# Second attention and both memory attentions by groups of four units, compressed branch ahead of it

## What is computed

```
# layer 0, per head (12), query tile of 128: keys 0..t, top-k mask
p = softmax(q_rot @ k.T * scale + mask);  o = p @ v
# both layers, memory heads (4), 256 keys, no mask
p = softmax(q_mem @ k_mem.T * scale);     o_mem = p @ v_mem
# layer 1 (NSA), per head (12), 2 groups of key heads
o_c = softmax(q    @ k_cmp.T * scale) @ v_cmp     # 31 compressed keys
o_s = softmax(q_rot @ k_s.T  * scale) @ v_s       # causal, all 8 blocks of 64 selected
o_w = softmax(q_rot @ k_w.T  * scale) @ v_w       # causal window of 512
o   = g0 * o_c + g1 * o_s + g2 * o_w              # g: sigmoid gates
x   = x + concat(o, o_mem) @ w_o
```

## Time and profile before

| | us |
|---|---|
| median of 3 runs (lowest, highest) | 2450.24 (2449.61, 2453.84) |
| profiled execution, its own time | 2453.7 |
| its span, first to last instruction | 2451.9 |
| PE busy | 2407.2 (98%) |
| ACT, POOL, DVE busy | 1070.1, 972.1, 912.3 |
| TensorE clock granted, mean | 0.997 |

### The profile page before, as it was taken

How to read it: one execution, slowest core, us unless ns; L and a number is a source line. 1 busy time by engine, 2 the same in 40 slices (tenths; PEclk the granted TensorE clock), 3 DMA queues, 4 the chain that set the end, 5 groups by cost and what they waited for, 6 DMA issues and landing times.

```text
span 2451.9 us, 36317 instructions
## 1 busy us (share of the span) xinstructions
PE 2407.2 (98%) x12294; PEld 1988.2 (81%) x12294; DVE 912.3 (37%) x1958; ACT 1070.1 (44%) x1853; POOL 972.1 (40%) x484
## 2 busy tenths in 40 slices
PE   8999999999999999999999999999999999999998
PEld 5888888888779978888887878788887797888886
DVE  7965322211567753222114243321211674221212
ACT  6565444422347744344335433432332583432321
POOL 4822444444331124444443413444443423444441
PEclk9999999999999999999999999999999999999999
DMA  4311222233320012322332212232222202232221
GB/s 155 112 36 40 95 98 95 94 103 105 120 69 1 1 45 93 103 94 94 107 107 79 92 38 82 74 103 94 94 96 93 69 18 69 86 103 94 94 95 68
DMA packets 57873, 202.85 MB, mean 83 GB/s; under 512 B 7072, under 2 KB 7968, under 8 KB 57392
## 3 DMA queue, kind: packets, MB, share of 16 engines
q1 hardware_dynamic: 54864, 196.02, 24.2%
q10 hardware_dynamic: 2912, 5.55, 0.7%
HBM read 199.44 MB, written 2.10 MB: 82 GB/s over the span
## 4 chain that ended last, share of the span: by engine, by line
PE 41%; issue 14%; POOL 7%; ACT 1%; DVE 1%; POOLq 0%; DVEq 0%; ACTq 0%
PE bank L804 36%; POOL w_lo L658 7%; PE bank L1058 1%; PE bank L1007 1%; ACT h_hi L1562 1%; PE bank L1442 0%; PE bank L1020 0%; PE bank L1423 0%; PE bank L1437 0%; ACT gained L1565 0%; PE bank L833 0%; ACT tmp L1661 0%; PE bank L838 0%; PE bank L921 0%; PE bank L810 0%
## 5 line engine op out<-in xcount | busy, mean ns | idle before, releaser
L658 POOL TENSOR_TENSOR w_lo<-w_raw,w_hi 128x1024 fp32r<-128x1024 f32 x368 | 883.4, 2401 | 1197.9 <-ACT w_hi L1519 1188.0
L804 PE MATMUL bank<-h_hi,w_hi 128*128 128x512 f32 x1648 | 651.4, 395 | 7.2 <-DVE tmp L2608 1.9
L804 PE MATMUL bank<-h_hi,w_lo 128*128 128x512 f32 x1648 | 643.5, 390 | 0.0
L804 PE MATMUL bank<-h_lo,w_hi 128*128 128x512 f32 x1648 | 643.3, 390 | 0.0
L1519 ACT ACTIVATE w_hi<-w_raw 128x1024 fp32r<-128x1024 f32 x368 | 386.8, 1051 | 241.2 <-PE bank L804 218.2
L804 PEld LDWEIGHTS bank<-h_hi,w_hi 128*128 128x128 f32 x1648 | 310.7, 189 | 82.6 <-issue 6.3
L804 PEld LDWEIGHTS bank<-h_lo,w_hi 128*128 128x128 f32 x1648 | 310.5, 188 | 65.3 <-issue 2.2
L804 PEld LDWEIGHTS bank<-h_hi,w_lo 128*128 128x128 f32 x1648 | 310.4, 188 | 65.3
L804 PE MATMUL bank<-mact_hi,w_hi 128*128 128x512 f32 x512 | 199.3, 389 | 1.7 <-DVEq L2471 1.7
L804 PE MATMUL bank<-mact_hi,w_lo 128*128 128x512 f32 x512 | 199.2, 389 | 0.0
L804 PE MATMUL bank<-mact_lo,w_hi 128*128 128x512 f32 x512 | 199.2, 389 | 0.0
(11 more groups left out here) (414 smaller groups left out, 3550.9 us busy)
## 6 DMA issues: line engine op xcount, KB each, us to landing
w_raw<-in_weights SPq DMA_DIRECT2D x368, 512.0 KB, 3.4
out<-x ACTq DMA_DIRECT2D x8, 256.0 KB, 2.1
x<-in_xT SPq DMA_DIRECT2D x4, 256.0 KB, 6.9
x<-in_xT ACTq DMA_DIRECT2D x4, 256.0 KB, 7.6
memx<-in_memT SPq DMA_DIRECT2D x1, 1024.0 KB, 9.8
cmp_w1k<-in_cmp_w ACTq DMA_DIRECT2D x1, 1024.0 KB, 4.8
cmp_w1v<-in_cmp_w ACTq DMA_DIRECT2D x1, 1024.0 KB, 7.0
rope_c<-in_rope_c SPq DMA_DIRECT2D x1, 256.0 KB, 8.4
```

Source lines behind the costliest of these rows:

```text
L658: nc.gpsimd.tensor_tensor(w_lo[:, t % RING, :], w_raw[:, t % RAW, :], w_hi[:, t % RING, :].bitcast(F32), ALU.subtract).then_inc(lo_ready, 1)
L804: r = nc.tensor.matmul(out, a, b, start=first and n == 0, stop=last and n == 2)
```

## The change

- The pair loop over `nsa0`, `nsa1` and `mem1` is gone. Layer 1's two causal branches become 24 **groups** of four units (a head's query tiles 0 and 3, or 1 and 2, each with both branches, so always 10 key tiles), run by the same functions as layer 0: `group_scores`, `group_transposes`, `group_values`, `group_output`. Values are made in row halves against 65 columns (`v_nsa` gets a column of ones).
- NSA's results of a group go scaled to a new tile `gated`, and POOL adds the two branches to `o_tok1` (`add_gated`, 2 instructions a group).
- The compressed branch of all 12 heads is made first, by pairs of heads, in a phase of its own (`compressed_attention` on PE, ACT and DVE), with its scores in place of the fillers and of the first NSA scores.
- A memory group is two heads times two query tiles instead of one head times four, in both layers, so that neighbouring score products lie in opposite row halves.
- Queries are read where they lie; POOL no longer copies them. It scales `q1` and `qmem` in place ahead of the attention (`compressed_queries_scaled`, `memory_queries_scaled`).
- ACT's order within a step changes from one exponential, two moves, three exponentials to two, two, two (both layers). `prob_groups` and `probT_groups` lie over `h_hi` and `h_lo`.

PE in layer 1's attention before: a piece of the loop's body (branch-2 units of two query tiles; `tmp` holds the exponentials, `sq` the transposed weights).

```diff
+def groups_of(kind):
+    if kind == "dsa":
+        return [[(head, qt, 1) for qt in range(TT)] for head in range(TOK_HEADS)]
+    if kind == "nsa":
+        return [[(head, qt, br) for qt in tiles for br in (1, 2)] for head in range(TOK_HEADS) for tiles in ((0, 3), (1, 2))]
+    return [[(2 * pair + hh, qt, 1) for qt in tiles for hh in range(2)] for pair in range(2) for tiles in ((0, 1), (2, 3))]
...
+            def memory_queries_scaled(l, queries, rstd):
+                for pair in range(2):
+                    wait_evacuated(pool, f"qmem{l}.{pair}")
+                    nc.gpsimd.tensor_tensor(queries[:, pair, :], queries[:, pair, :], rstd[:, :], ALU.mult).then_inc(mem_q_scaled, 1)
+            def compressed_queries_scaled(p):
+                pool.wait_ge(roped, 8 + p)
+                nc.gpsimd.tensor_tensor(q1[:, p, :], q1[:, p, :], rstd_nsa[:, :], ALU.mult).then_inc(q1_scaled, 1)
+            def add_gated(k):
+                units = group(1, k)
+                head, first, second = units[0].head, units[0].qt, units[2].qt
+                out = o_tok1[:, first:second + 1:second - first, head * HD:head * HD + HD]
+                src = gated[:, k % 2, :, :].rearrange("p (a b) n -> p a b n", a=2)
+                pool.wait_ge(cmp_out, head + 1)
+                pool.wait_ge(gated_made, k + 1)
+                for b in range(2):
+                    if b:
+                        pool.wait_ge(gated_added, 2 * k + 1)
+                    nc.gpsimd.tensor_tensor(out, out, src[:, :, b, :], ALU.add).then_inc(gated_added, 1)
...
+            def group_scores(unit):
+                rows, l, pair = slice(HD * (unit.head % 2), HD * (unit.head % 2) + HD), int(unit.kind == "mem1"), unit.head // 2
+                queries, out = slice(unit.qt * P, (unit.qt + 1) * P), score_bank[unit.n % 4]
+                n = P * len(key_tiles(unit.kind, unit.qt))
+                if unit.n >= 4:
+                    pe.wait_ge(probs_ready, unit.n - 1)
+                if unit.kind.startswith("mem"):
+                    pe.wait_ge(mem_scaled, l + 1)
+                    pe.wait_ge(mem_q_scaled, 2 * l + pair + 1)
+                    nc.tensor.matmul(out[:, 0:n], (qmem0, qmem1)[l][rows, pair, queries], k_mem[rows, l, pair, :],
+                                     start=True, stop=True).then_inc(scores_ready, 1)
+                    return
+                if unit.kind == "dsa":
+                    q, ks = q_dsa, [k[:, 0:n] for k in k_dsa]
+                else:
+                    q, ks = q_nsa, [k[:, 2 * (unit.branch - 1) + unit.head // 6, 0:n] for k in k_nsa]
+                for part, k in enumerate(ks):
+                    r = nc.tensor.matmul(out[:, 0:n], q[:, unit.head, queries], k, start=part == 0, stop=part == 1)
+                r.then_inc(scores_ready, 1)
+            def group_transposes(unit):
+                pe.wait_ge(probs_ready, unit.n + 3)
+                pe.wait_ge(probT_ready[unit.n % 2], unit.n // 2 + 1)
+                weights = in_group(prob_groups, unit)
+                for n in range(len(key_tiles(unit.kind, unit.qt))):
+                    part = slice(n * P, (n + 1) * P)
+                    r = nc.tensor.transpose(probT_bank[unit.n % 2][:, part], weights[:, part], ident[:, :])
+                r.then_inc(transposed, 1)
+            def group_values(units):
+                if units[0].n >= 8:
+                    pe.wait_ge(o_done, units[0].n - 2)
+                for place, unit in enumerate(units):
+                    pe.wait_ge(probT_ready[unit.n % 2], unit.n // 2 + 2)
+                    weights, kts = in_group(probT_groups, unit), key_tiles(unit.kind, unit.qt)
+                    for n, kt in enumerate(kts):
+                        if unit.kind == "dsa":
+                            v = dsa_v[:, kt, :]
+                        elif unit.kind == "nsa":
+                            v = v_nsa[:, kt, 2 * (unit.branch - 1) + unit.head // 6, :]
+                        else:
+                            v = v_mem[:, int(unit.kind == "mem1"), kt, unit.head, :]
+                        for rows in (slice(0, HD), slice(HD, P)):
+                            r = nc.tensor.matmul(group_sums(unit.n)[rows, place, :], weights[:, n * P + rows.start:n * P + rows.stop], v,
+                                                 start=n == 0, stop=n == len(kts) - 1)
+                    r.then_inc(pv_done, 1)
+            def transposes_around_scores(stream, turned, scored):
+                for unit in group(stream, turned)[0:2]:
+                    group_transposes(unit)
+                for unit in group(stream, scored):
+                    group_scores(unit)
+                for unit in group(stream, turned)[2:4]:
+                    group_transposes(unit)
+            def attention_by_groups(stream):
+                transposes_around_scores(stream, 0, 1)
+                for k in range(len(GROUPS[stream])):
+                    group_values(group(stream, k))
...
+            def compressed_attention(begin):
+                pairs = TOK_HEADS // 2
+                for p in range(2):
+                    compressed_scores(p)
+                compressed_transposes(0)
+                for p in range(pairs):
+                    if p + 2 < pairs:
+                        compressed_scores(p + 2)
+                    if p + 1 < pairs:
+                        compressed_transposes(p + 1)
+                    if p == pairs - 1:
+                        begin(0)
+                    compressed_values(p)
+                begin(1)
...
+                        if half == 0:
+                            pe.wait_ge(cmp_shifted, TOK_HEADS // 2)
+                            pe.wait_ge(q_split, 24)
+                        else:
+                            pe.wait_ge(cmp_out, TOK_HEADS - 2)
...
+            def moves_and_exponentials(stream, moved, weighed):
+                for unit in group(stream, moved)[1:2]:
+                    group_move(unit)
+                for unit in group(stream, weighed)[0:2]:
+                    group_exponentials(unit)
...
+            def group_output(stream, k):
+                units = group(stream, k)
+                n, kind, head, qt, _, _ = units[0]
+                sums, four = group_sums(n), slice(n % 8, n % 8 + TT)
+                inverse = rinv[:, four].rearrange("p (a b) -> p a b", b=1).to_broadcast([P, TT, HD])
+                dve.wait_ge(pv_done, units[-1].n + 3)
+                if kind == "nsa":
+                    step_of = units[2].qt - qt
+                    gate = gates[:, qt:units[2].qt + 1:step_of, 3 * head + 1:3 * head + 3]
+                    nc.vector.tensor_tensor(oscale[:, four].rearrange("p (a b) -> p a b", a=2), sums[:, :, HD].rearrange("p (a b) -> p a b", a=2), gate,
+                                            ALU.mult).then_inc(oscale_ready, 1)
+                    dve.wait_ge(oscale_ready, 2 * k + 1)
+                    nc.vector.reciprocal(rinv[:, four], oscale[:, four]).then_inc(oscale_ready, 1)
+                    dve.wait_ge(oscale_ready, 2 * k + 2)
+                    if k >= 2:
+                        dve.wait_ge(gated_added, 2 * (k - 1))
+                    nc.vector.tensor_tensor(gated[:, k % 2, :, :], sums[:, :, 0:HD], inverse, ALU.mult).then_inc(o_done, TT)
+                    dve.wait_ge(o_done, units[-1].n + 3)
+                    dve.sem_inc(gated_made, 1)
+                    return
...
+            def compressed_maxima(p):
+                src = score_bank[p % 2][:, 0:2 * P].rearrange("p (a c) -> p a c", c=32)
+                dve.wait_ge(cmp_scored, p + 1)
+                if p >= 2:
+                    dve.wait_ge(cmp_shifted, p - 1)
+                nc.vector.tensor_reduce(c_max[:, p % 2, :, 0], src, AX.X, ALU.max).then_inc(cmp_reduced, 1)
```

More of the change, by code:

```diff
@@ L168, in attention_unit, with numbered @@
+def numbered(kind):
+    groups, n = [], UNIT0[kind]
+    for places in groups_of(kind):
+        units, start = [], 0
+        for head, qt, branch in places:
+            end = start + P * len(key_tiles(kind, qt))
+            units.append(Unit(n, kind, head, qt, branch, slice(start, end)))
+            n, start = n + 1, end
+        groups.append(units)
+    return groups
 def attention_unit(kind, u):
-    if kind.startswith("nsa"):
-        hh, r = divmod(u, 9)
-        return (hh, NSA_ORDER[(r - 1) // 2], 1 + (r - 1) % 2) if r else (hh, 0, 0)
@@ L174, in attention_unit @@
     return u // 4, u % 4, 1
-def compressed(kind, u):
-    return kind.startswith("nsa") and u % 9 == 0
 def slot_of(kind, u):
-    return u % (9 if kind.startswith("nsa") else 8)
+    return u % 8
 def look_ahead(kind):
[L188 to L202, removed]
@@ L205, in prob_columns @@
[L205 to L214, removed]
+    return 5
 def bank_of(kind, u):
[L219 to L221 removed]
+    return u % 4
 def attention_stream(eng, passes, begin, pair_of_heads, first=None):
@@ L1291, in _ @@
             pe.wait_ge(q_split, 12)
-            def banks_free():
```

(16 more changed lines are left out.)

621 lines of the change are left out of this document (275 added, 346 removed).

## The result

The changed kernel takes 2424.16 us (median of 4, 2423.8 to 2425.16), beside 2451.62 us (median of 4) for the kernel before in the same set: ratio 0.9893, 95% interval 0.9881 to 0.9905. The forecast was 2422.5, in a range of 2417 to 2429.

The account below looks back on a forecast made before the run. PE, busy 98% of the span, was taken as the bound. Layer 1's attention 25.0 us and layer 0's 2.8 shorter: 2453.7 to 2425.9, less 3.5 for the profiled execution's excess over the median: 2422.5 us, range 2417 to 2429.

Parts of the forecast that it names:

- 24 groups at layer 0's pace: Layer 1's NSA groups: each takes 3.89 us like a layer-0 head, 85.5 us from first values to group 22's.
- Rival (1): Layer 1's NSA groups miss layer 0's pace by 0.2 us each: +4.8, 2427.3 us; chance 0.13.
- (4): Layer 1's attention: clock stays at 1.2 GHz for long, column tiles half filling the array; +52, 2475 us; chance 0.02.
- (5): Unrolled code or its waits cost a microsecond per group, nothing is left: 2450 us; chance 0.03.
- Value halves, 0.065 us a tile: Layer 1's value products in row halves save 0.065 us a tile, 15.6 us over 240 tiles.
- The compressed phase: Layer 1 before the groups: DVE sets the pace, 1.45 us per output; first values at 749.65, 751.0 with POOL's delay.
- I add one POOL instruction, 1.27: Compressed phase: DVE's gates instructions wait for one POOL instruction, 1.27 us rounded to 1.35.
- at no cost: Changes priced at nothing: POOL's missing query copies, the w_lo chunk and SP's next weight load, `v_nsa`'s ones.
- Memory groups: Both layers: paired scores save 0.87 us per block, 6.9 over eight, part given back to the loop through the engines.
- Rival (2), row halves give nothing: Memory steps stay near 4.2 us because ACT and DVE free the banks: +5.6, 2428 us; chance 0.10.
- Rival (3), the clock: Compressed phase: PE's waits bring clock falls, 1.5 us each; two give 2426 us; chance 0.10.
- The sum: Both layers' gains together: -27.8 us, 2453.7 to 2425.9 for the profiled execution, median 2422.5.

Follow-up runs that it names:

- act_one: Changed kernel with ACT's old order (one exponential, two moves, three exponentials) in all groups; 2420.31 us, ratio 0.9878.
- whole: Changed kernel with NSA values as whole products of 128 query rows instead of two halves of 64; 2439.13 us, ratio 0.9959.
- after_again: The changed kernel as it is, run and profiled once more; 2424.26 us, ratio 0.9894.
- late: Changed kernel with POOL's w_lo chunk moved from after the memory queries' scaling to behind the fourth NSA group's addition; 2419.43 us, ratio 0.9883.
- one_head: Changed kernel with memory groups of one head and four query tiles again, in both layers; 2429.27 us, ratio 0.9914.
- best: Changed kernel with the edits of `late` and `act_one` together; 2418.79 us, ratio 0.9875.
- best_early: `best` with group 0's first two score units one step earlier in the compressed phase; 2418.74 us, ratio 0.9878.
- best_max: `best_early` with DVE's maxima of group 0's first two units ahead of the last compressed output, PE's wait moved to first values; 2417.31 us, ratio 0.9867.

## Why the prediction was right, and where its terms were off

The time, the sign and the main mechanisms, value halves and row halves, came out as forecast. That the time came within 2 us is in part luck: terms were off both ways and cancelled. By its own steps:

*24 groups at layer 0's pace.* 3.91 us instead of 3.89; 0.5 us in 22. Of the 0.02, ACT's order holds nearly all (3.89 in `act_one`). Rival (1) is out, and with it (4) and (5): the 22 groups ran at 1.00 and without an idle record. Groups of tiles 0 and 3 and of tiles 1 and 2 differ, 4.09 and 3.73 us, which the mean hid.

*Value halves, 0.065 us a tile.* 0.070 by `whole`. The rows gave 0.205 - 0.144 = 0.061, rounded up on the way. "The rest is the compressed branch and PE's changes between kinds of products" was wrong: of layer 1's 24.1 us, 17.1 came up to `mem1`'s first values, where value halves gave 16.8 and row halves 1.6, so that block order and compressed phase together gave nothing; and 7.0 came in the memory heads, which the forecast had not compared with the units before.

*The compressed phase.* The forecast for the first values, 751.0 less 729.23 = 21.8 us after the first scores, met the 21.82 of `after_again`, but by luck, by two errors that cancel. "DVE is thus the chain" was wrong: without the lock the phase and ramp take 19.79 us, not 749.65 - 729.23 = 20.4, because DVE's output of a pair takes 1.17 us and not 1.45, and PE's 2.05 a pair is then the longer; its sign "DVE without gaps" failed too, by waits for PE of 0.23 to 1.01 us, one of 0.69 even in `late`. And "I add one POOL instruction, 1.27" took the wrong one: the gates met the w_lo chunk of 2.35 us, which stands in the forecast's list "at no cost", so 2.0 to 2.2 were lost instead of 1.35. I had taken the length of the scaling without asking which of POOL's instructions would stand beside the gates.

*Memory groups.* "Eight records take four slots": 0.86 of the 0.87 measured, 1.06 for 1.92. "ACT's new order puts the second exponential ahead of the moves, which makes this loop" is shown by `act_one`: 3.60 with it, 3.32 without. What was mis-sized is the last step, which I left at 2.68: its values wait in the same loop, 2.97. Together with 3.93 for 3.82 in layer 1 and 3.83 for 3.70 in layer 0, each layer gave 0.4 us less than forecast: layer 0 gained 2.4 us (from 2.8), layer 1's part 17.8 where 17.4 was summed.

*Rival (2), row halves give nothing.* Out, by `one_head`: 4.9 us. The rule weighed there, that evacuation may become the bottleneck where tiling speeds up the products (the Trainium skill, TensorEngine Tiling (Array Packing), Performance Considerations), describes what was left in part: with ACT's order as changed, the loop through ACT and not PE set the step, at 3.60 and not near 4.2. It was the length of the loop and not its load, for ACT was busy for 12.99 and DVE for 12.24 of the 19.77 us.

*Rival (3), the clock.* It took place in the first profile (one fall, 23.36 - 21.82 = 1.5 us, as priced) and not in the second. So the change doesn't bring it each time.

*The sum.* Without falls in the stretches compared, layer 0 gained 2.4 us and layer 1 151.73 - 127.63 = 24.1, 26.5 in all, where the forecast had 27.8. Subtracted from 2450.24 that is 2423.7; the median measured was 2424.16. The forecast took off as a constant the 3.5 us by which the first profile of before stood above its median. At 1.7 us a fall these are two falls more than an execution at the median had; that is worked out, not shown, since the median's executions have no trace here.

What stays open: what decides whether the clock falls at a given place. `late`, `best`, `best_early` and `best_max`, with the shorter wait in the compressed phase, had no fall there in four executions; the six executions of changed kernels with the long wait or the fillers had five. That speaks for a part of the phase's idle time in it, but four against six executions don't show it.

## What to carry to other kernels

Price a product by the distance between starts in the trace, and look there for how its neighbours are laid on the array: independent products over 64 rows that alternate row halves took little more than half as long, and values in two halves of 64 columns of the array a third less than whole ones. Once PE's step has become shorter, write down the loop through the other engines again and take out of it whatever may stand later; here one exponential of 0.35 us moved behind two moves gave 2.6 us in the two layers. And when work is moved together on POOL, look which of its instructions stands beside each short SBUF instruction of DVE that the next stage waits for, and give it the length of that one.

## What the runs showed of the hardware that was not expected

The clock's falls are not fixed to the code. At 92 to 94 us every kernel has the same gap of PE, 2.51 to 2.53 us, waiting for POOL; the windows behind it, of the changed kernel in its first and its second profile:

```profile
95.80:98.00 2.20, 2.20 (x20) 2.20 (x20) 0.93 (x4) 0.04 (x1) 2.17 (x2) 1.00 0.63 223
```

and in the second:

```profile
95.80:98.00 2.20, 2.20 (x13) 2.20 (x12) 0.99 (x2) 0.00 (x0) 2.06 (x3) 0.50 0.72 238
```

The same code ran 20 products at 1.00 once and 13 at 0.50 the other time. Layer 0's first values stand at 149.6 us in the two profiles without this fall (`whole` is the other) and at 150.7 to 151.3 in all with it. I had read the first as a gain of ACT's new order. Over all profiles an execution has two to five such falls, about 1 to 1.7 us each: a difference of some 5 us between two single profiles of this kernel says nothing until the falls are counted.
